# Forming the second part of a modulation vector with GpSimd products and ScalarE sums in place of TensorE matmuls

## The reference, cut to what matters

```python
mod_ctx = (silu(c_ctx) @ w_ada + b_ada)      # w_ada: 1024 x 6144
mod_lat = (silu(c)     @ w_ada + b_ada)
sh1, sc1, g1, sh2, sc2, g2 = split(mod, 6)
h   = rms_norm(x, norm1_g) * (1 + sc1) + sh1
mix = mixer_block(h)                         # h @ w_in, attention, gated delta rule, output projections
x   = x + g1 * mix
h2  = rms_norm(x, norm2_g) * (1 + sc2) + sh2
out = x + g2 * ((silu(h2 @ w_gate) * (h2 @ w_up)) @ w_down)
```

## Time and profile before

| | |
|---|---|
| device time, median of 3 runs | 2724.4 us (2722.95 to 2741.44) |
| span of the profiled execution | 2733.5 us |
| PE busy in it | 2537.5 us (93%) |
| DVE, ACT, POOL busy | 1709.1, 1231.2, 625.1 us (63, 45, 23%) |
| mean granted TensorE clock | 0.958 |
| DMA | 357.63 MB, mean 131 GB/s |

### The profile page before, as it was taken

The page is one execution under the profiler, slowest core; times in us unless marked ns, Lnnn a source line. Parts: engine busy times, 40 slices in busy tenths (PEclk is TensorE's granted clock), DMA queues, the critical chain, the costliest instruction groups (busy, mean ns, idle before and its releaser), DMA issues. The chain is left out here.

```text
span 2733.5 us, 45747 instructions
## 1 busy us (share of the span) xinstructions
PE 2537.5 (93%) x17286; PEld 2387.3 (87%) x17286; DVE 1709.1 (63%) x2810; ACT 1231.2 (45%) x2225; POOL 625.1 (23%) x558
## 2 busy tenths in 40 slices
PE   6999999969998999985999998989999999999999
PEld 3899999958887888884778777989999999999999
DVE  3666332146676577745988883446886664777776
ACT  4322344233433334323888883344653333545443
POOL 1000222243443343313563544332000000000000
PEclk9999999978998899975999999999999999999999
DMA  5322666343335333314111004632335551537764
GB/s 219 139 86 94 203 220 205 127 130 90 94 103 164 96 110 92 84 31 140 55 39 63 17 13 136 241 136 94 120 107 177 191 187 66 175 105 249 261 223 150
DMA packets 238032, 357.63 MB, mean 131 GB/s; under 512 B 85984, under 2 KB 161792, under 8 KB 236288
## 3 DMA queue, kind: packets, MB, share of 16 engines
q1 hardware_dynamic: 234944, 339.11, 38.0%
q10 hardware_dynamic: 2880, 15.73, 1.7%
HBM read 262.66 MB, written 92.09 MB: 130 GB/s over the span
## 5 line engine op out<-in xcount | busy, mean ns | idle before, releaser
L277 PE MATMUL proj_ps<-h_hi,w_hi 128*128 128x320 f32 x896 | 282.9, 316 | 6.0 <-DVE w_lo L575 5.6
L277 PE MATMUL proj_ps<-h_lo,w_hi 128*128 128x320 f32 x896 | 278.2, 310 | 0.0
L277 PE MATMUL proj_ps<-h_hi,w_lo 128*128 128x320 f32 x896 | 277.9, 310 | 0.0
L1079 ACT ACTIVATE x_inv<-banks_bc 128x1024 fp32r<-128x1024 f32 x120 | 122.7, 1025 | 275.3 <-PE banks_bc L1213 274.5
L2276 DVE TENSOR_TENSOR mf_up_slots<-mf_up_raw,mf_up_slots 128x512 fp32r<-128x512 f32 x198 | 137.3, 694 | 117.9 <-ACT mf_up_slots L2251 117.7
L277 PEld LDWEIGHTS proj_ps<-h_hi,w_hi 128*128 128x128 f32 x896 | 169.7, 189 | 7.1 <-DVE w_lo L575 3.3
L277 PEld LDWEIGHTS proj_ps<-h_lo,w_hi 128*128 128x128 f32 x896 | 169.7, 189 | 0.0
L277 PEld LDWEIGHTS proj_ps<-h_hi,w_lo 128*128 128x128 f32 x896 | 169.5, 189 | 0.0
L3049 PE MATMUL f_ps_b<-mf_t_r,mf_up_slots 128*128 128x320 f32 x1056 | 166.0, 309 | 3.2 <-DVE mf_sg L2964 3.2
L3049 PE MATMUL f_ps_b<-mf_t_s,mf_up_slots 128*128 128x320 f32 x1056 | 166.6, 310 | 2.0 <-PEq L2281 2.0
L3049 PE MATMUL f_ps_c<-mf_t_s,mf_up_slots 128*128 128x320 f32 x1056 | 166.3, 310 | 0.0
(11 more groups left out here) (395 smaller groups left out, 6880.5 us busy)
## 6 DMA issues: line engine op xcount, KB each, us to landing
mf_up_raw<-w_up_dram SPq DMA_DIRECT2D x33, 1024.0 KB, 5.0
w_raw<-w_in_dram SPq DMA_DIRECT2D x48, 512.0 KB, 4.3
mf_down_raw<-down_sums SPq DMA_DIRECT2D x32, 704.0 KB, 4.4
mf_down_raw<-w_down_dram SPq DMA_DIRECT2D x24, 704.0 KB, 4.5
w_ada_raw<-w_ada_dram SPq DMA_DIRECT2D x16, 1024.0 KB, 5.0
mf_w_raw<-w_mix_dram SPq DMA_DIRECT2D x30, 512.0 KB, 5.0
f_t<-mf_c SPq DMA_DIRECT2D x44, 320.0 KB, 2.4
delta_t<-delta_tile ACTq DMA_DIRECT2D x10, 1024.0 KB, 6.7
```

Source lines behind the costliest of these rows:

```text
L277: ins = nc.tensor.matmul(out, w(k), a(k), start=(first and n == 0 and q == 0), stop=(last and n == len(ks) - 1 and q == 2))
L1079: nc.scalar.activation(XX[:, c].rearrange("p t h i -> p t (h i)"), BC[c][:], ACT.Copy).then_inc(e["x_ready"], 1)
```

## The change

The matrix for the last 32 modulation tiles is given to the kernel transposed (`w_ada_t`: one row of 1024 per output), and the two conditioning vectors as rows (`c_rows`), which a DMA copies to all 128 partitions. ACT takes their Silu once. Then, for each modulation tile and each conditioning vector, POOL multiplies the 128x1024 tile with the row (`n` counts these products, 64 in all), and ACT copies the product onto itself with an accumulated sum, which is the output column. Product `n` for c = 0 goes to one scratch tile `wprod`, so it waits for the sum of n - 2; for c = 1 it overwrites the weights. Two load buffers replace one. The matmuls, the transposes, the fp32r split of `w_ada` and of `c`, and the copy of the rows are gone. ACT does two sums after group 2 of each tile (behind the copy of `cols`) and two after group 0 of the next one (behind `squares`).

```diff
-        wr = sb("w_ada_raw", [P, 2, KT, P])
-        wh = sb("w_ada_hi", [P, 2, KT, P], F32R)
-        wl = sb("w_ada_lo", [P, 2, KT, P], F32R)
-        c4 = sb("c_hi_lo", [P, KT, 4], F32R)
-        mrow = sb("mod_rows2", [4, 2, P])
+        wt = sb("w_ada_rows", [P, 2, 2, D])
+        c_rows = sb("c_rows", [P, 2, D])
+        wprod = sb("w_ada_products", [P, D])
...
+        ada_products = lambda n: wt[:, n // 4 % 2, n // 2 % 2] if n % 2 else wprod[:]
...
-            sp.dma_start(wr[:], io["w_ada"][ADA1:ADA1 + 2].rearrange("u p k n -> p u k n")).then_inc(ada_in, 16)
+            sp.dma_start(c_rows[:].rearrange("p c k -> p (c k)"), io["c_rows"].rearrange("c k -> (c k)").partition_broadcast(P)).then_inc(c_rows_in, 16)
+
+            def load_ada(a):
+                if a >= 2:
+                    sp.wait_ge(ada_done, 4 * a - 4)
+                sp.dma_start(wt[:, a % 2], io["w_ada_t"][2 * a:2 * a + 2].rearrange("u p k -> p u k")).then_inc(ada_in[a % 2], 16)
+
+            load_ada(0)
...
                 if t < LAST:
-                    sp.wait_ge(ada_lo, a + 1)
-                    sp.dma_start(wr[:], io["w_ada"][ADA1 + 2 * a + 2:ADA1 + 2 * a + 4].rearrange("u p k n -> p u k n")).then_inc(ada_in, 16)
+                    load_ada(a + 1)
...
-            for a in range(FILL0 - CONV_TILES):
-                pool.wait_ge(ada_hi, a + 1)
-                if a:
-                    pool.wait_ge(ada_done, a)
-                nc.gpsimd.tensor_tensor(wl[:], wr[:], wh[:].bitcast(F32), ALU.subtract).then_inc(ada_lo, 1)
+            pool.wait_ge(c_rows_ready, 1)
+            for n in range(2 * ADA2):
+                a, u, c = n // 4, n // 2 % 2, n % 2
+                if n % 4 == 0:
+                    pool.wait_ge(ada_in[a % 2], 16 * (a // 2) + 16)
+                if c:
+                    pool.wait_ge(ada_product, n)
+                elif n:
+                    pool.wait_ge(ada_done, n - 1)
+                nc.gpsimd.tensor_tensor(ada_products(n), wt[:, a % 2, u], c_rows[:, c], ALU.mult).then_inc(ada_product, 1)
...
-            def ada_split(a):
...
-            def ada_out(a):
...
+            def ada_sums(a, u):
+                for c in range(2):
+                    n = 4 * a + 2 * u + c
+                    act.wait_ge(ada_product, n + 1)
+                    nc.scalar.activation(ada_products(n), ada_products(n), ACT.Copy, accum_out=keep["mod"][:, ADA1 + n // 2, c:c + 1]).then_inc(ada_done, 1)
...
                 split_hi(t + 1, (t + 1) % 2, (t + 1) // 2 + 1)
-                if a:
-                    ada_out(a - 1)
-                ada_split(a)
+                if t == CONV_TILES:
+                    act.wait_ge(c_rows_in, 16)
+                    silu(c_rows[:], c_rows[:]).then_inc(c_rows_ready, 1)
...
                     if g == 2 and j is not None:
                         cols(j, 0)
+                    if g == 0 and t > CONV_TILES:
+                        ada_sums(t - CONV_TILES - 1, 1)
+                    if g == 2:
+                        ada_sums(t - CONV_TILES, 0)
...
-            ada_out(LAST - CONV_TILES)
+            ada_sums(LAST - CONV_TILES, 1)
...
-            dve.wait_ge(ada_turned, ADA2 // 2)
-            nc.vector.tensor_tensor(mod[:, ADA1:], mod_ps[:, :, 0:2], keep["b_ada"][:, ADA1:].unsqueeze(2).to_broadcast([P, ADA2, 2]), ALU.add).then_inc(mod_ready, 1)
+            dve.wait_ge(ada_done, 2 * ADA2)
+            nc.vector.tensor_tensor(mod[:, ADA1:], mod[:, ADA1:], keep["b_ada"][:, ADA1:].unsqueeze(2).to_broadcast([P, ADA2, 2]), ALU.add).then_inc(mod_ready, 1)
...
-            def ada(a):
...
-            def ada_turn(a):
...
-        "w_ada": tiles_of(a["w_ada"][0]),
+        "w_ada": tiles_of(a["w_ada"][0][:, :ADA1 * P]),
+        "w_ada_t": a["w_ada"][0].T[ADA1 * P:].reshape(ADA2, P, D),
+        "c_rows": np.stack([a["c_ctx"], a["c"][0]]),
```

More of the change, by code:

```diff
@@ L308, in in_projection @@
         qn = lambda j: padded[:, j % 2, 0:512]
-        row_ps, col_ps, ada_ps = ps[4:7], ps[6], ps[7]
-        mod_ps = ps[3][:, GN:GN + 4 * ADA2].rearrange("p (t c) -> p t c", c=4)
+        row_ps, col_ps = ps[4:7], ps[6]
         cum_ps = [ps[6 + d][:, GN:GN + 160].rearrange("p (a j h) -> p a j h", a=2, h=8) for d in range(2)]
@@ L318, in in_projection @@
         conv_tap, silu_done, conv_sc = sem("conv_tap"), sem("silu_done"), sem("conv_sc")
-        ada_in, c_split, ada_hi, ada_lo, ada_done, ada_rows, ada_turned, mod_ready = (
-            sem(n) for n in ("ada2_in", "c_split", "ada2_hi", "ada2_lo", "ada2_done", "ada2_rows", "ada2_turned", "mod2_ready"))
+        c_rows_in, c_rows_ready, ada_product, ada_done, mod_ready = (sem(n) for n in ("c_rows_in", "c_rows_ready", "ada2_product", "ada2_done", "mod2_ready"))
+        ada_in = [sem("ada2_in0"), sem("ada2_in1")]
         tile_in = [sem("tile_in0"), sem("tile_in1")]
@@ L467, in conv @@
                     nc.scalar.activation(stage[:, p], acc[:, p], ACT.Silu).then_inc(silu_done, 1)
-            def ada_split(a):
-                act.wait_ge(ada_in, 16 * a + 16)
-                if a:
-                    act.wait_ge(ada_done, a)
-                cp(wh[:], wr[:]).then_inc(ada_hi, 1)
-            def ada_out(a):
[L476 to L479, removed]
+            def ada_sums(a, u):
[3 more added lines that the diff above has]
+                    nc.scalar.activation(ada_products(n), ada_products(n), ACT.Copy, accum_out=keep["mod"][:, ADA1 + n // 2, c:c + 1]).then_inc(ada_done, 1)
             def squares(j):
@@ L501, in rest @@
             def rest(t):
-                a, j = t - CONV_TILES, delta_of(t)
+                j = delta_of(t)
                 if t > DR0 and delta_of(t - 1) is not None:
@@ L518, in rest @@
                         cols(j, 0)
+                    if g == 0 and t > CONV_TILES:
+                        ada_sums(t - CONV_TILES - 1, 1)
+                    if g == 2:
+                        ada_sums(t - CONV_TILES, 0)
             split_hi(0, 0, 1, False)
-            cp(c4[:, :, 0:2], keep["c_act"][:]).then_inc(c_split, 1)
             scalars_a()
             phases(act, conv, rest)
-            ada_out(LAST - CONV_TILES)
+            ada_sums(LAST - CONV_TILES, 1)
             for p in range(2):
@@ L634, in _ @@
             split_lo(0, 0, False)
-            dve.wait_ge(c_split, 1)
-            nc.vector.tensor_tensor(c4[:, :, 2:4], keep["c_act"][:], c4[:, :, 0:2].bitcast(F32), ALU.subtract).then_inc(c_split, 1)
             scalars_a()
@@ L642, in _ @@
             mod = keep["mod"]
-            dve.wait_ge(ada_turned, ADA2 // 2)
-            nc.vector.tensor_tensor(mod[:, ADA1:], mod_ps[:, :, 0:2], keep["b_ada"][:, ADA1:].unsqueeze(2).to_broadcast([P, ADA2, 2]), ALU.add).then_inc(mod_ready, 1)
+            dve.wait_ge(ada_done, 2 * ADA2)
+            nc.vector.tensor_tensor(mod[:, ADA1:], mod[:, ADA1:], keep["b_ada"][:, ADA1:].unsqueeze(2).to_broadcast([P, ADA2, 2]), ALU.add).then_inc(mod_ready, 1)
             dve.wait_ge(mod_ready, 1)
-            nc.vector.tensor_tensor(mod[:, ADA1:], mod_ps[:, :, 2:4], mod[:, ADA1:], ALU.add).then_inc(mod_ready, 1)
-            dve.wait_ge(mod_ready, 2)
             nc.vector.scalar_tensor_tensor(keep["mod_scale"][:, 1], mod[:, 32:40], 1.0, keep["gains"][:, 1].unsqueeze(2).to_broadcast([P, KT, 2]), ALU.add, ALU.mult)
@@ L735, in rest @@
                         rows(j)
[L736 to L741, removed]
+                    if g == 2 and j is not None:
+                        cols(j, 0)
                     if g == 3 and j is not None:
@@ L745, in _ @@
             phases(pe, conv, rest)
-            ada_turn(LAST - CONV_TILES)
 LEVELS = 7
```

## The result

| | kernel before | changed kernel |
|---|---|---|
| device time, median | 2729.2 us (2722.95 to 2741.44, 4 runs) | 2689.4 us (2681.41 to 2691.43, 4 runs) |
| ratio, 95% interval | | 0.9841 (0.981 to 0.9873) |
| span of the profiled execution | 2733.5 us | 2687.1 us |
| the stage: first matmul of tile 0 to first matmul of the next stage | 472.7 us (80.44 to 553.13) | 429.8 us (81.58 to 511.41) |

The kernel is 1.6% faster by this ratio (the two medians alone are 39.8 us, 1.5%, apart); 2682 us had been forecast, with 42.7 us gained in the stage. The stage is 42.86 us shorter. The stage is the better ruler of the two: from its end to the end of the span the kernels before and after took 2180.4 and 2175.7 us, and over all traces shown here, none of which changes anything there, this stretch lies between 2166.1 and 2181.2.

A forecast was written before the change was run, and what follows sets the result against it. PE's own queue was taken to set the stage's length. Removed matmuls, turns and tile 12's pause give 42.6 us, less 0.8 for `conv_tile`, plus 0.9 at the end: 42.7 us, median 2724.4 to 2681.7 us; range 2674 to 2698.

The forecast's parts named there:

- PE's queue is the bound, and what leaves it is gained whole: Tiles 13 to 27: PE busy 266.8 of 268.0 us, so removed matmuls shorten delta tiles from 18.55 to 16.27 us.
- Tile 12, 10.2 us, and the clock: Before group 3 of tile 12: products and PE's pause go, 9.85 us, plus 0.36 from the lower clock behind the pause.
- First `conv_tile`, a wait of 0.8 us (bounds 0.8 to 7.5): Tile 13: PE, arriving earlier, newly waits 0.8 us at `rows` for this load, up to 7.5 if other transfers slow it.
- Rival 2: Tile 13: the first `conv_tile` is late, costing 7.5 us in place of 0.8, giving 2688.4 us; chance 0.08.
- Durations on POOL and ACT: A product takes 2.38 us on POOL, a sum 1.06 + 0.19 on ACT; ACT rises to some 10 us a tile.
- `L609` near 0.16 us in delta tiles: DVE's small step after `squares`, 1.71 us when behind POOL, finds POOL idle; the chain gets up to 1.5 us shorter.
- Rival 1: Delta tiles: DVE, POOL and ACT hold each other up, 1.5 to 2.4 us a tile, giving 2697 to 2706; chance 0.12.
- `split_lo` may stretch, with slack for it: This DVE step now meets a product on POOL; 1 us allowed for a meeting, against 10 us of slack.
- The end, 9.0 us after group 2 (bounds 8.0 to 11.2): From tile 27's group 2 to the next stage: 8.3 us of work plus 0.7 for the block exit, 9.9 before.
- Sum, 42.7 us: Whole stage: 42.6 from PE, less 0.8 for `conv_tile`, plus 0.9 at the end; median 2724.4 to 2681.7 us.
- Rival 3: Products and sums without overlap become the bound, 14.5 us a tile; slower when a product passes 3.4 us, 2738; chance 0.04.
- Rival 4: Later stages: PE's clock or `delta_scan` interleaving gives back half, 21 us, leaving 2703 us; chance 0.05.

The follow-up runs named there:

- experiment 1: Kernel before without PE's modulation matmuls and turns and ACT's row copy, nothing in their place; loads, ACT's split and POOL's subtraction stay: stage 435.0 us, ratio 0.9866.
- experiment 7: Changed kernel with each product and sum in one DVE instruction, none on POOL or ACT: stage 430.9 us, ratio to before 0.9849.
- Experiment 3: Kernel before with ACT's first modulation split moved from tile 12 to behind tile 1: stage 466.1 us, ratio 0.9983.
- experiment 5: Changed kernel with ACT's two sums after group 0 put ahead of `squares`: stage 432.9 us, median 2682.3 us (1 run).
- Experiment 4: Changed kernel with every even product made twice (stage 452.7 us, ratio 0.9923) or three times (stage 516.0 us, median 2779.5 us) on POOL.
- experiment 2: Kernel of experiment 1 with a second load buffer, POOL writing its result over ACT's copy: stage 432.1 us, ratio to before 0.9842.

## Why the prediction was right

- *PE's queue is the bound, and what leaves it is gained whole.* Right. Delta tiles were forecast at 16.27 us and are 16.26. Experiments 1 and 7 show it from both sides: with nothing in place of the matmuls, and with another engine for them, the stage is within 5.2 and 1.1 us of the changed kernel's, and the 5.2 are one wait in tile 13.
- *Tile 12, 10.2 us, and the clock.* Right: no pause, granted clock 1.00 where it was 0.76. Experiment 3 gained 6.6 us with the pause alone gone and 1.6 us lost to a wait of its own, together 8.1 of the 8.3 that were expected there.
- *First `conv_tile`, a wait of 0.8 us (bounds 0.8 to 7.5).* 0.70. It landed 5.1 us after its issue again (271.74 to 276.85), though 1 MB was issued behind it at 272.18 and the DMA share in this stretch is 1.01. Rival 2 fell. Over the traces of this case the first transfer took 4.9 to 5.8 us; that the queue serves it ahead of the others, which the prediction gave as the reason, no run shows by itself.
- *Durations on POOL and ACT.* 2.41 to 2.44 for 2.38; 1.05 + 0.19 for 1.06 + 0.19. ACT is busy 132.94 of 223.0 us, 9.2 of a mean tile of 15.5, for a forecast of some 10.
- *`L609` near 0.16 us in delta tiles.* Right in nine of ten (0.17, now `L616`); 0.71 in tile 13, where the first products came late and the step ends with one (281.50 against 281.48). Rival 1 fell, and experiment 5 shows that its price was too high besides. Its room of 1.35 us, from 10.5 to 11.85, was read with one blocked step already inside. In the changed kernel the scaled rows of tile 19 are ready at 380.10, 9.2 us into the tile, and PE starts on them at 382.82: 2.7 us of room. In experiment 5, with the step blocked and `squares` moved back, 0.3 of them are left in tiles 18 and 19, and nine tiles of ten lose nothing.
- *`split_lo` may stretch, with slack for it.* It does: 1.87 us in the mean and 2.87 at most against 1.22, and PE never waits for it.
- *The end, 9.0 us after group 2 (bounds 8.0 to 11.2).* 8.34. The mis-sized term is the exit from the block, taken as 0.7: DVE ends at 511.09 and PE starts at 511.41, 0.3 us. The work ahead of the exit took 8.0 us for 8.3.
- *Sum, 42.7 us.* 42.86 in the stage: 0.7 better at the end, 0.5 worse over the rest, of which 0.2 lie ahead of the end of group 2 in tile 12, where nothing was changed. That these two nearly cancel is luck, of a few tenths of a microsecond. The ratio forecast, 2682 to 2724.4, is 0.9844, measured 0.9841. That the median is 2689.4 and not 2682 is no effect of the change: the kernel before has 2729.2 us here, not the 2724.4 of the first three runs, off which the forecast would be 2686.5, and the other 3 us are inside the spread of the runs.
- *Rival 3, the chain of products and sums as the bound.* It fell for the changed kernel, yet its working was wrong. It took 14.5 us a tile without overlap, put the point of decision at a product of 3.4 us, and priced what lay beyond at +24. Experiment 4 shows the chain with three products in a pair at 16.3 us a tile, mostly overlapped: 22.9 us worse than the changed kernel and still 20.0 better than before. By its line the gain begins to go at 14.9 us a tile, below PE's own mean tile, and is gone at 17.6, by estimate products of 4.4 us and not 3.4.
- *Rival 4.* Nothing was given back behind the stage: 2175.7 and 2179.8 us in the two traces of the changed kernel, 2180.4 before, within the scatter of the other traces.

## What to carry to other kernels

Where one engine is busy without a gap, a piece of work moved off it is worth its time in that engine's own queue, here to a few tenths of a microsecond, and twice the total work elsewhere costs nothing as long as it fits there (9.7 us of POOL in a mean tile of 15.5 here; by the line of experiment 4 the gain begins to go at 14.9). Read the price from the distances between the instructions around it, and price the pause that its first input causes by itself. Then look for the one place where the receiving engine's instruction can lie beside a short step of another engine that the bound waits for: here the order on ACT (sums behind `squares`) kept 4.8 us of POOL off ten small DVE steps. Compare the receiving engine's whole time per tile with the tile as it will be, not as it was.

## What the runs showed of the hardware

- A DVE subtraction of 128x1024 with two SBUF inputs took 1.22 us with POOL empty and 4.69 us when a POOL instruction of 4.63 us was under way; a 128x8 step on DVE took 0.17 against 1.4 to 2.1. It works the other way as well: the longest of POOL's products, 3.28 us for 2.41, began at 278.20 when a DVE subtraction (277.95 to 279.20) had 1.0 us to go. The Trainium skill, SBUF — State Buffer, Who interferes with whom, says that such instructions of these two engines block each other whole; the trace agrees: the subtraction of 4.69 us ended 1.1 us after POOL's instruction, which is nearly its own 1.22.
- PE's granted clock was 0.57 over the four us behind a wait of 4.38 us in tile 13 (experiment 1) and 1.00 behind one of 2.52 us in the same place (experiment 2). The lower clock cost 1.8 us.
- DVE's product with accumulated sum took 1.22 + 0.08 us for 128x1024 fp32, half of POOL's product alone.
- The change of block took 0.3 us where a compute instruction ended last (511.09 to 511.41). Where a store was last, the next stage began 3.3 us after its issue (507.65 to 510.90), in the kernel before 3.6 (549.52 to 553.13).
- The 768 KB of the first `conv_tile` landed 5.1 us after their issue though 1 MB was issued right behind them (DMA share 1.01); in the kernel before, with that load 3.7 us behind, it was 5.1 us too, and over all traces 4.9 to 5.8. The 1 MB load of experiment 2, issued 2.4 us earlier than in experiment 1, landed 0.6 us earlier.
